# A chunked delta-rule stage in another order: key tiles first, one exponential for gates and norms, one bank per chunk

## What is computed

```
p = h @ w_in            # gate_in, gate_out, a_h, q k v, z, beta, alpha
qkv = silu(causal_dwconv(qkv, dn_conv_w))             # width 4
q = l2_norm(q) * 128 ** -0.5 ; k = l2_norm(k)         # x * rsqrt(sum(x * x) + eps)
beta = sigmoid(beta_raw)
g = -exp(a_log) * softplus(alpha_raw + dt_bias)
decay = cumsum(g) in a chunk ; dmask[i, j] = exp(decay[i] - decay[j]), j <= i
A = I + strict(beta[i] * (k_i . k_j) * dmask)
u = inv(A) @ (beta * v) ; w = inv(A) @ (beta * exp(decay) * k)
chunk by chunk:  v_new = u - w @ S
                 o = (q * exp(decay)) @ S + (incl(q k^T) * dmask) @ v_new
                 S = S * exp(decay_last) + (k * exp(decay_last - decay))^T @ v_new
o = rms_norm(o) * silu(z)
y_a = gate_out * causal_dwconv(gate_in * a_h, conv_a_w)   # width 3
mix = concat(y_a, o) @ w_out
```

## Time and profile before

| | |
|---|---|
| median of three runs | 1309.52 us (1309.21 to 1311.0) |
| the profiled execution | 1310.43 us |
| its span | 1308.6 us |
| TensorE busy | 1260.2 us (96%), 10253 matmul records |
| VectorE busy | 894.0 us (68%) |
| ScalarE busy | 661.2 us (51%) |
| GpSimd busy | 181.3 us (14%) |

### The profile page before, as it was taken

One profiled execution on the slowest core, in us unless ns is written; L12 is line 12 of the kernel. 1 busy time (PEld: TensorE's weight loads), 2 busy tenths in 40 slices (PEclk: granted clock), 3 DMA queues, 4 the chain that ended last, 5 costly groups with the idle time before them and its releaser, 6 DMA issues.

```text
span 1308.6 us, 27282 instructions
## 1 busy us (share of the span) xinstructions
PE 1260.2 (96%) x10253; PEld 1221.0 (93%) x10253; DVE 894.0 (68%) x1677; ACT 661.2 (51%) x1168; POOL 181.3 (14%) x207
## 2 busy tenths in 40 slices
PE   7987999999999998999999999999999989999996
PEld 7867999999999887999999999999999978999996
DVE  6966437877854786888854776967555797876443
ACT  6554224555533564655543655655444476655331
POOL 0113405000011333200011000500011103100111
PEclk9988989999999998999999999999999999999998
DMA  7431114876654323655664443666566622665651
GB/s 257 149 97 56 59 49 125 226 201 193 206 180 142 127 82 116 197 186 182 206 202 154 146 141 113 203 185 190 180 190 185 219 65 92 199 188 181 191 182 63
DMA packets 60659, 206.32 MB, mean 158 GB/s; under 512 B 6176, under 2 KB 14624, under 8 KB 60448
## 3 DMA queue, kind: packets, MB, share of 16 engines
q1 hardware_dynamic: 56256, 200.81, 49.2%
q10 hardware_dynamic: 4320, 4.35, 1.1%
HBM read 200.95 MB, written 4.19 MB: 157 GB/s over the span
## 4 chain that ended last, share of the span: by engine, by line
PE 89%; DVE 7%; ACT 2%; issue 1%; DMA 0%; POOL 0%; DVEq 0%; POOLq 0%; ACTq 0%
PE bank L309 26%; PE bank L311 26%; PE bank L310 26%; DVE w_lo L266 1%; DVE cb L663 1%; PE bank L1329 1%; PE bank L1352 1%; PE bank L1342 1%; PE bank L1175 1%; PE bank L1193 1%; PE bank L1191 1%; DVE sm_d L1370 1%; ACT w_hi L257 1%; PE bank L1129 1%; DVE sm_d L1392 0%
## 5 line engine op out<-in xcount | busy, mean ns | idle before, releaser
L266 DVE TENSOR_TENSOR w_lo<-raw,w_hi 128x1024 fp32r<-128x1024 f32 (+1 forms) x358 | 459.1, 1283 | 210.0 <-ACT w_hi L257 209.1
L257 ACT ACTIVATE w_hi<-raw 128x1024 fp32r<-128x1024 f32 (+1 forms) x358 | 387.5, 1085 | 305.8 <-PE bank L311 282.1
L309 PE MATMUL bank<-x_hi,w_hi 128*128 128x256 f32 (+2 forms) x1784 | 516.2, 289 | 11.3 <-DVE x_lo L393 8.0
L311 PE MATMUL bank<-x_hi,w_lo 128*128 128x256 f32 (+2 forms) x1784 | 509.6, 286 | 0.0
L310 PE MATMUL bank<-x_lo,w_hi 128*128 128x256 f32 (+2 forms) x1784 | 509.5, 286 | 0.0
L309 PEld LDWEIGHTS bank<-x_hi,w_hi 128*128 128x128 f32 x1784 | 339.4, 190 | 15.5 <-DVE w_lo L266 10.5
L311 PEld LDWEIGHTS bank<-x_hi,w_lo 128*128 128x128 f32 x1784 | 339.7, 190 | 0.0
L310 PEld LDWEIGHTS bank<-x_lo,w_hi 128*128 128x128 f32 x1784 | 338.9, 190 | 0.3
L309 PE MATMUL bank<-m_hi,w_hi 128*128 128x256 f32 x512 | 143.4, 280 | 0.0
L310 PE MATMUL bank<-m_lo,w_hi 128*128 128x256 f32 x512 | 142.8, 279 | 0.0
L311 PE MATMUL bank<-m_hi,w_lo 128*128 128x256 f32 x512 | 142.8, 279 | 0.0
(11 more groups left out here) (312 smaller groups left out, 1745.3 us busy)
## 6 DMA issues: line engine op xcount, KB each, us to landing
raw<-w_up SPq DMA_DIRECT2D x88, 512.0 KB, 3.9
raw<-w_mlp_up SPq DMA_DIRECT2D x64, 512.0 KB, 3.5
raw<-w_mlp_down SPq DMA_DIRECT2D x64, 512.0 KB, 3.7
raw<-w_down SPq DMA_DIRECT2D x32, 704.0 KB, 4.1
raw<-w_mix_in SPq DMA_DIRECT2D x29, 512.0 KB, 3.6
raw<-w_moba_in SPq DMA_DIRECT2D x24, 512.0 KB, 4.1
raw<-w_swa_in SPq DMA_DIRECT2D x12, 512.0 KB, 3.5
raw<-w_mix_out SPq DMA_DIRECT2D x8, 512.0 KB, 3.5
```

Source lines behind the costliest of these rows:

```text
L257: nc.scalar.activation(w_hi[:, slot, 0:WIDTHS[g]], raw[:, slot, 0:WIDTHS[g]], ACT.Copy).then_inc(hi_ready, 1)
L266: nc.vector.tensor_tensor(w_lo[:, slot, 0:WIDTHS[g]], raw[:, slot, 0:WIDTHS[g]], w_hi[:, slot, 0:WIDTHS[g]].bitcast(F32), ALU.subtract).th ...
L309: nc.tensor.matmul(out, whi, xh, start=(chunk == 0), stop=False)
L311: mm = nc.tensor.matmul(out, wlo, xh, start=False, stop=end)
```

## The change

- The tiles of `mix_in` come in another order: four key tiles with a convolution, and between them the four z tiles and the rates (tiles 0 to 8); then the queries (9 to 12), the values (13 to 16) and the triples as before (17 to 28). Tiles from 9 on use banks 0 and 1 in turn, so that tile t waits until tile t - 2 is read. The weights are laid out in this order on the host.
- `mix_slots` and its loop are gone: all slots are written out.
- beta is no longer made: its logarithm, min(raw, 0) - log(1 + exp(-|raw|)), stands in rows 32 to 35 of `ba`, the sum of squares' logarithm in rows 64 to 67 (keys) and 96 to 99 (queries). A product with the constant `sel` adds decay, log beta and -1/2 log norm, broadcast over the partitions; one exponential with the column's sum as bias gives the factor of every pair (a_t for the keys, qk_t for the queries), and VectorE multiplies it into the key or query products in one instruction, with a bound of 2e6. The strict mask falls away, since the masks of the levels contain it. Column factors come from nine small products and three exponentials (`cexp`, `glast`). q and k themselves are not scaled any more.
- Each chunk has one bank for the whole inverse (`INV`), in which both results of a level are packed side by side, and every level is followed by two projection tiles, one after each half.
- The scan runs among tiles 23 to 28.

```diff
@@ constants, banks
-        INV_BANKS = {1: (bank[0][:, :], bank[5][:, :], bank[6][:, :]),
-                     2: (bank[1][:, :], bank[7][:, :], bank[2][:, :]),
-                     0: tuple(bank[4][:, 4 * META * i:4 * META * (i + 1)] for i in range(3))}
-        BC = (bank[0], bank[1], bank[2], bank[7])
...
+        K_TILES, BA, Z_TILES, Q0, V0, GLU0 = (0, 2, 4, 6), 5, (1, 3, 7, 8), 9, 13, 17
...
+        LARGE = 2e6
...
+        BC = (bank[7], bank[2], bank[3], bank[7])
+        K_ROWS = {1: bank[2], 2: bank[3], 0: bank[7]}
...
+        INV = {0: bank[4], 1: bank[5], 2: bank[6]}
@@ tile_bank
-            if lin is LIN["mix_in"] and t >= A0_TILE:
-                return bank[BANKS - 1]
+            if lin is LIN["mix_in"] and t >= Q0:
+                return bank[t % 2]
@@ dve_mix
+                nc.vector.scalar_tensor_tensor(out=a_t[0:c, n, 0:w], in0=a_t[0:c, n, 0:w], scalar=LARGE,
+                                               in1=KK[n][0:c, 0:w], op0=ALU.min,
+                                               op1=ALU.mult).then_inc(S("a_t_ready"), 1)
...
+            for t in range(4):
+                rest(t)
+            dve_rstd(dve, name)
+            evict_conv(0)
+            evict_z(0)
+            conv(0, between=1)
...
+            gate_val(1)
+            dve.wait_ge(S("l2_sum"), 2)
+            y_low(dve, "mix_out", 0, av[:, 0, :])
+            rest(GLU0 + 4)
+            for n in chunks_at(6):
+                x_next(6, n)
@@ act_mix
+            act_link(act, nc.scalar.activation(g1[:, :], braw[:, :], ACT.Abs, bias=prm_col("dt_bias", 0, 36)))
+            nc.scalar.activation(small[0:4, 0:1], prm_col("a_log", 0, 4), ACT.Exp)
+            act_link(act, nc.scalar.activation(g1[:, :], g1[:, :], ACT.Exp, scale=-1.0))
+            nc.scalar.activation(g2[:, :], g1[:, :], ACT.Ln, bias=1.0).then_inc(S("gates_act"), 1)
...
+                    ins = nc.scalar.activation(a_t[0:c, n, hd * c:(hd + 1) * c], BC[hd][0:c, t0:t0 + c], ACT.Exp,
+                                               bias=colsb[0:c, n, hd:hd + 1])
+                ins.then_inc(S("expa_ready"), 1)
...
+            rows(kd, K_ROWS, 0, 3, 8)
+            silu(6)
+            for n in chunks_at(2):
+                p_copy(2, n)
@@ pe_mix
+            for t in range(4, 9):
+                tile(t)
+            pe.wait_ge(S("rel_ready"), 1)
+            l2_sums(0, 64)
+            tile(Q0)
+
+            pe.wait_ge(S("rows_ready"), 4)
+            pe.wait_ge(S("ls_ready"), 1)
...
+            for n in chunks_at(3):
+                first(3, n)
+            tile(V0 + 1)
+            for n in chunks_at(3):
+                second(3, n)
```

More of the change, by code:

```diff
@@ L345, in pe_linear @@
                 pe_tile(pe, lin, t, ready=ready if t == 0 else None)
[L346 to L354, removed]
+                if t == 0 and name in NORMS:
                     norm_sum(pe, name)
@@ L621, in build @@
+        O_SPREAD = (bank[5], bank[4], bank[7])
         LEVELS = {0: 4, 1: 7, 2: 7}
+        CHUNKS = (1, 2, 0)
         MIX_EARLY = 3
         o_std, o_rec = small[:, 40:52], small[:, 52:64]
[L624 to L625 removed]
         bt_ready = [S(f"bt_ready{n}") for n in range(3)]
@@ L1270, in pe_mix, with tile, part @@
-            side_part(15, 5, 8)
+            def tile(t):
+                pe_tile(pe, lin, t, ready=ready if t == 0 else None)
+            def part(t, a, b):
+                pe_tile(pe, lin, t, part=(a, b))
+            for t in range(3):
+                tile(t)
+            pe.wait_ge(S("ones_loaded"), 16)
+            norm_sum(pe, name)
+            tile(3)
+            pe.wait_ge(loaded, 16)
+            nc.tensor.matmul(bank[7][0:HEADS, 0:VLEN],
+                             prm[0:BUCKETS, PARAM_AT["rel"][0]:PARAM_AT["rel"][0] + HEADS],
+                             C("onehot", BUCKETS), start=True, stop=True).then_inc(S("rel_done"), 1)
@@ new lines, in pe_mix @@
+            rows(0, K_ROWS, 4)
+            for n in CHUNKS:
+                turn(n)
+            tile(Q0 + 2)
+            for n in chunks_at(2):
+                first(2, n)
+            tile(Q0 + 3)
+            for n in chunks_at(2):
+                second(2, n)
+            tile(V0)
+            for n in chunks_at(3):
+                first(3, n)
+            tile(V0 + 1)
+            for n in chunks_at(3):
+                second(3, n)
+            pe.wait_ge(S("rows_read"), 3)
+            l2_sums(4, 96)
@@ new lines, in pe_mix @@
+            tile(V0 + 2)
+            for n in chunks_at(4):
+                first(4, n)
+            tile(V0 + 3)
+            for n in chunks_at(4):
+                second(4, n)
+            pe.wait_ge(S("ls_ready"), 2)
+            for hd in range(3):
+                broadcast(hd, 20, S("bcq_done"))
+            tile(GLU0)
+            for n in chunks_at(5):
+                first(5, n)
+            pe.wait_ge(S("expq_ready"), 1)
+            broadcast(3, 20, S("bcq_done"))
+            tile(GLU0 + 1)
@@ new lines, in pe_mix @@
+            for n in chunks_at(5):
+                second(5, n)
+            pe.wait_ge(S("mix_silu"), 12)
+            pe.wait_ge(xt_ready[0], LEVELS[0])
+            rows(0, V_ROWS, 8)
+            tile(GLU0 + 2)
+            tile(GLU0 + 3)
+            for n in chunks_at(6):
+                first(6, n)
+            pe.wait_ge(S("expq_ready"), 4)
+            for n in CHUNKS:
+                gram(n, QK, 0, S("gram_q"))
+            tile(GLU0 + 4)
+            for n in chunks_at(6):
+                second(6, n)
@@ new lines, in pe_mix @@
+            pe.wait_ge(S("qk_t_ready"), 2)
+            rows(1, V_ROWS, 8)
+            rows(2, V_ROWS, 8)
+            tile(GLU0 + 5)
+            for n in chunks_at(7):
+                first(7, n)
+            pe.wait_ge(S("rows_read"), 6)
+            new_values(0)
+            tile(GLU0 + 6)
+            state_step(0)
+            outputs(0)
+            second(7, 1)
+            keys_state(1)
+            second(7, 2)
+            tile(GLU0 + 7)
+            new_values(1)
+            part(GLU0 + 8, 0, 3)
```

1048 lines of the change are left out of this document (563 added, 485 removed).

## The result

The changed kernel takes **1292.75 us** (median of four runs, 1290.53 to 1298.23) beside 1309.37 us for the kernel before on the same chip (four runs, 1308.49 to 1311.0): a ratio of 0.9873, 95% interval 0.986 to 0.9885. The forecast was 1292, with a range of 1283 to 1302, and faster. The profiled execution is the slowest of the four, 1298.23 us with a span of 1296.4; its mean granted clock is 0.981, that of the other three 0.987 to 0.990. The profiled execution therefore shows more low clock than the others had.

The account below looks back on a forecast made before the run. TensorE was taken to bound the stage, losing time to gaps, low clock and slow matmul pace. A 30.9 us ceiling minus 13.5 (6.5 waits, 2.5 hand-offs, 4.5 clock) left 17.4 us gained: 1292 us, range 1283 to 1302.

Parts of the forecast that it names:

- The ceiling: Stage up to mix_out's chunk 4: at most 30.9 us to gain, 28.9 lost by TensorE plus 2.0 less work.
- (a): Head: four roundings before the square root expose its table load, so the fifth tile starts 0.4 us late.
- (b): Gates before the column products: rows ready at 46.3 us, leaving TensorE 1.6 us idle where 3.2 were.
- (c): Fourth broadcast waits for a bank that three exponentials read, after a table load: 0.5 us.
- (d): Level 2: copies of P stand on ScalarE behind the third query tile's silu, leaving TensorE 2.0 us idle.
- (e): Level 6: VectorE's y_low stands behind four scaled row copies, 0.9 us.
- (f): End of the stage: the last y_lo comes 1.1 us after TensorE is ready, 0.9 before.
- The clock: Two clock falls of 3.4 to 6.8 us, behind the gates' wait and where chunk 0 meets level 7: 4.5 us.
- R1: Rival, slower: from tile 9 two banks tie TensorE to VectorE's reads and the clock keeps falling: 1320 us, chance 0.04.
- R2: Rival: the level-2 wait on ScalarE's queue repeats at levels 3 to 6, 2 us four times: 1300 us, chance 0.22.
- R3: Rival, better: denser tiles keep the stage's clock up and the walk's waits halve: 1284 us, chance 0.18.
- R4: Rival, no change: time saved earlier is only waited for at the scan's end: 1309 us, chance 0.02.

Follow-up runs that it names:

- state-first kernel: Changed kernel with ScalarE's level-2 copies of P earlier, tile GLU0 + 6 split around chunk 0's state products, and VectorE's state copy ahead of that tile's eviction: 1286.15 us.
- early copies: Changed kernel with the level-2 copies of P placed ahead of chunk 0's key rows and the third query tile's silu on ScalarE: 1285.22 us.
- root early: Changed kernel with the norm's square root ahead of ScalarE's fourth rounding, and VectorE's reciprocal and two evictions ahead of its fourth rest: 1295.68 us.
- copies and root together: Changed kernel with both the early level-2 copies of P and the early square root: 1286.62 us.
- all of it: The state-first kernel with the early square root and the early rounding of the first y added: 1286.96 us.

## Why the prediction was right, and where it was not

- **The ceiling, 28.9 us lost and 2.0 of work: right.** The state-first kernel ends the stage 28.5 us earlier than before with 3.4 us of waits left and no low clock: 31.9 against 30.9. The broadcasts run twice fit their price, and nine column products took 48.42 − 46.66 = 1.8 us where 1.9 were taken.
- **The new waits, 6.5 us: right in sum (6.6), wrong in parts,** so that the sum is in part luck. (a) was 1.6, not 0.4. Beside the table load of 1.28 us, the roundings ahead of the root had waited 1.66 us for a weight transfer, which the walk didn't price (its rows stand with those of the table loads below). (b), 1.6 us before the column products, didn't come: the late tile head used it up, and rows were ready at 46.5, with TensorE there at 46.66. (c) didn't come as a wait of its own. (d) was 2.7 us, not 2.0, and by the queue order given; what made it longer is that VectorE's three taps took 2.58 us there, beside GpSimd's masking, against 1.57 us one slot later. (e) was 1.1 and (f) 0.5. The level-1 turns, 0.7, were not in the list. The 2.5 us for hand-offs were not needed.
- **The clock, 4.5 us: the step that was mis-sized.** The text put the falls behind (b) and where chunk 0 meets level 7, 3.4 to 6.8 us each. There were four stretches, 27.2 us. Taken from the difference to the state-first kernel, 189.91 − 176.42 = 13.5, less 6.6 − 3.4 = 3.2 us of waits, they cost about **10.3 us** (an estimate: the two kernels also differ in where one tile and one copy stand). The largest, 13.6 us long, stands behind the wait (d) that I had found, and to which I gave no fall. I also valued low clock at half its length; a tile in it takes 5.51 us against 3.12, which is 2.4 in 5.5. (PEclk reads 1.00 at that first tile, but its products start 0.227 us apart, as they do in the low stretch from 144.9 us.)
- **The sum.** Forecast 30.9 − 13.5 = 17.4 for the stage, found 15.0: the clock cost 5.8 more than its term, the 2.5 for hand-offs were not needed, and the ceiling was 1.0 too low. The stage ended at 189.9 us, where about 187 was named. 2.8 more went behind it. So the profiled execution was 5.2 us over the 1293.0 of the sum. The median lies on the forecast because the other three executions had a higher mean clock than the profiled one (0.987 to 0.990 against 0.981). That part was luck.
- **Packing and cover.** Packing at nothing: shown. Two tiles a level cover the hand-offs: shown between levels 2 and 3, by taking the tile away there.
- **The table loads.** Here, too, a load takes 1.28 us and the next instruction follows it after 0.01 us:

```profile
40.75 1.28 ACT L1009 ACT_TABLE_LOAD   x1
42.04 0.20 ACT L1009 ACTIVATE small<-prm 4x1 f32<-4x1 f32 x1
...
42.58 1.28 ACT L1011 ACT_TABLE_LOAD   x1
43.88 0.43 ACT L1011 ACTIVATE g<-g 36x272 f32<-36x272 f32 x1
```

And in the head, with the rounding that waited for its weights:

```profile
17.17 1.06 ACT L258 ACTIVATE w_hi<-raw 128x1024 fp32r<-128x1024 f32 x1 [1.66 <-DMA raw<-w_mix_in]
...
20.76 1.28 ACT L366 ACT_TABLE_LOAD   x1
22.06 0.49 ACT L366 ACTIVATE std<-bank,eps 128x272 f32<-128x272 f32 x1
```

The Trainium skill (ScalarE: Activation LUTs, What ACT_TABLE_LOAD costs) states 1.28 us for the load and 2.66 us a switch with a drain. The first agrees with these rows, the second does not: no row beside a load shows the drain.
- **The rivals.** R1 did not happen; even with one bank the loss is 4.3 us, not the 28 of R1. The two-bank stretch from 83.66 to 142.53 us has a clock of 1.00. So the oscillation that the Trainium skill describes for cycling banks (TensorE: Matmul & The Clock Gate, A second HAM failure mode: psum-queue depth-cycling) is not seen there. R2 did not happen: pb is waited for at level 2 alone. R3, 1284, is about what the early copies give (1285.22). R4, no change, did not happen.

## What to carry to other kernels

When a walk through the queues finds a wait of 2 to 3 us on a TensorE that is otherwise full, price the low clock behind it too; here it cost twice the wait (5.7 beside 2.7 us), and moving ScalarE's copies ahead of a silu that waited for another engine gave back 7.5 us. When a tile is moved to fill a hole, look at which of the other engines' queued steps stand behind its eviction: the filler can become what is waited for. And once a stage is nearly full, its executions differ by where the clock falls, so small edits are judged by several runs with their clocks, not by one profile.

## What was not expected of the hardware

- In six kernels (the changed one and five of the experiments) the wait at level 2 was 2.5 to 2.7 us; each profile shows a low stretch with it, 6.8 to 13.6 us long, which begins between 0.8 us before and 2.3 us after the wait's end, though TensorE is then busy throughout with 64-column products and a tile. With no wait there (five kernels) none has one, with 1.5 us (one profile) none either; with the 3.33 us wait it lasted 10.2 us, from 70.5 us on, while that wait still ran. What sets its length stays open.
- Before the fifth tile, waits of 1.4 to 2.0 us were each followed by a low stretch of 3.4 us (five profiles), waits of 1.1 or 1.2 us by none (five profiles). The length of the wait does not decide everywhere: at the column products a wait of 0.5 us was followed by a low stretch of 3.4 us in two profiles (root early, copies and root together) and by none in a third (all of it).
- The granted clock also falls at 430 and 1050 us, in code that is the same in both kernels, in some kernels' profiles and not in others.
- Three taps on VectorE took 2.58 us at 67.22 us, where GpSimd was masking blocks until 68.91 us, and 1.57 us at 73.41 us, when GpSimd was idle:

```profile
64.93 3.98 POOL L1153 TENSOR_TENSOR bt<-a_t,cst 128x512 f32<-128x512 f32 x3
```

```profile
73.41 1.57 DVE L664 SCALAR_TENSOR_TENSOR cb<-gb,prm,cb 128x272 f32<-128x272 f32 x3
```
